# A second, turned copy of the prompt in place of TensorE transposes, in a one-core RG-LRU and HGRN2 layer

## What is computed

```
hn = rmsnorm(x, pre_w) * (1 + scale) + shift       # over D = 1024
xa, ga, q, fr, iv, gb = split(hn @ w_in)           # 6 x 512 columns
ya = rglru(causal_conv(xa)) * silu(ga)             # group A
yb = rmsnorm(hgrn2(q, log f, k, v=iv)) * silu(gb)  # group B, 4 heads of 128
x  = x + gate * rmsnorm(concat(ya, yb) @ w_out, post_w)
```

## Time and profile before

| what | us |
|---|---|
| median of 3 timed runs (lowest to highest) | 954.21 (952.94 to 954.56) |
| profiled execution | 949.82 |
| span of the profiled execution | 948.0 |
| TensorE (PE) busy | 883.1 (93% of the span) |
| VectorE (DVE) busy | 681.3 (72%) |
| ScalarE (ACT) busy | 510.7 (54%) |
| GpSimd (POOL) busy | 259.5 (27%) |

### The profile page before, as it was taken

How to read it: one execution, slowest core, us unless ns; L and a number is a source line. 1 busy time by engine, 2 the same in 40 slices (tenths; PEclk the granted TensorE clock), 3 DMA queues, 4 the chain that set the end, 5 groups by cost and what they waited for, 6 DMA issues and landing times.

```text
span 948.0 us, 20981 instructions
## 1 busy us (share of the span) xinstructions
PE 883.1 (93%) x8178; PEld 650.4 (69%) x8235; DVE 681.3 (72%) x1791; ACT 510.7 (54%) x1057; POOL 259.5 (27%) x348
## 2 busy tenths in 40 slices
PE   5889948899999999999999999999999999999884
PEld 5648847468675877579666877588757966697742
DVE  3586795768677776867686877778686768587766
ACT  2665468434763367536753377436852575436531
POOL 6031345602242222313140224212241214032400
PEclk9999987999999999999999999999999999999997
DMA  9965111100110010100110011001010101010234
GB/s 364 386 255 209 46 45 45 67 2 24 46 68 1 24 46 24 45 4 21 45 68 1 24 46 67 2 23 46 20 49 1 47 1 53 2 46 1 73 107 139
DMA packets 21821, 61.19 MB, mean 65 GB/s; under 512 B 2844, under 2 KB 11888, under 8 KB 18140
## 3 DMA queue, kind: packets, MB, share of 16 engines
q1 hardware_dynamic: 21724, 59.86, 17.0%
HBM read 48.90 MB, written 10.95 MB: 63 GB/s over the span
## 4 chain that ended last, share of the span: by engine, by line
PE 53%; DVE 20%; ACT 14%; issue 8%; DMA 2%; POOL 2%; SPq 0%; DVEq 0%; ACTq 0%; POOLq 0%
PE ring L429 43%; DVE xc L1347 5%; DMA work<-in_ada_w_dram 2%; DVE qlo L1250 2%; DVE kk L1268 2%; ACT hnh L1000 2%; ACT okv L997 2%; DVE qq L1266 1%; PE okv L518 1%; ACT L972 1%; ACT aux L997 1%; ACT wih L1024 1%; PE okv L520 1%; PE okv L519 1%; DVE xc L1345 1%
## 5 line engine op out<-in xcount | busy, mean ns | idle before, releaser
L429 PE MATMUL ring<-hnh,wih 128*128 128x256 bf16 (+1 forms) x1152 | 288.9, 262 | 2.4 <-DVE hnl L1389 2.2
L429 PE MATMUL ring<-hnl,wih 128*128 128x256 f16 (+1 forms) x1152 | 288.8, 262 | 0.0
L429 PE MATMUL ring<-hnh,wil 128*128 128x256 bf16 (+1 forms) x1152 | 288.8, 262 | 0.0
L429 PE MATMUL ring<-woh,work 128*128 128x512 f16 x512 | 162.4, 379 | 1.3
L1772 POOL TENSOR_TENSOR klo<-kk,khi 128x256 bf16<-128x256 f32 x96 | 75.3, 784 | 227.6 <-ACT khi L912 227.2
L429 PEld LDWEIGHTS ring<-hnh,wih 128*128 128x128 f16 x1152 | 109.8, 98 | 15.4 <-DVE hnl L1389 2.8
L429 PEld LDWEIGHTS ring<-hnl,wih 128*128 128x128 f16 x1152 | 109.8, 98 | 11.9
L429 PEld LDWEIGHTS ring<-hnh,wil 128*128 128x128 bf16 x1152 | 109.8, 98 | 11.5
L1250 DVE TENSOR_TENSOR qlo<-qq,qhi 128x256 f16<-128x256 f32 x112 | 66.5, 593 | 67.1 <-ACT qhi L916 57.7
L912 ACT ACTIVATE khi<-kk 128x256 f16<-128x256 f32 x96 | 40.4, 421 | 115.3 <-DVE kk L1268 90.6
L429 PE MATMUL ring<-wih,hnh 128*128 128x512 f16 x256 | 97.1, 379 | 2.4 <-ACT kk L895 1.3
(11 more groups left out here) (356 smaller groups left out, 1905.2 us busy)
## 6 DMA issues: line engine op xcount, KB each, us to landing
xin<-in_x_prompt_dram SPq DMA_DIRECT2D x16, 512.0 KB, 3.6
work<-in_x_prompt_dram SPq DMA_DIRECT2D x16, 512.0 KB, 4.2
out_dram<-work SPq DMA_DIRECT2D x16, 512.0 KB, 2.6
work<-in_ada_w_dram SPq DMA_DIRECT2D x4, 1024.0 KB, 7.5
woh<-in_ada_w_dram SPq DMA_DIRECT2D x4, 1024.0 KB, 12.2
wol<-in_w_in_dram SPq DMA_DIRECT2D x4, 1024.0 KB, 13.5
work<-in_w_in_dram SPq DMA_DIRECT2D x4, 1024.0 KB, 10.1
woh<-in_w_in_dram SPq DMA_DIRECT2D x4, 1024.0 KB, 9.6
```

The lines of the kernel that those rows point to most:

```text
L429: last = mm(out, a(k), b(k), start=start and k == ks[0] and j == 0, stop=stop and k == ks[-1] and j == 2)
```

## The change

- The host puts a second layout of the prompt in memory, `x_turned`: for each body 128 partitions (columns of a block of D) by 8 x 256 tokens. From body 1 on, SyncE loads it into `xin` by one DMA of 1 MB (`load_turned`), and TensorE transposes no rows. Body 0 works as before.
- The rows are still needed for the sums of squares. They come in four parts of 128x512 through a small buffer `xs` of two parts (`load_part`); for body 1 the second tile lands in `gp`, which is free until the gate's rows are written there.
- The factors lie one to a token. `spread` makes two matmuls with a stationary operand that repeats a column of factors 128 times, and ident as the moving one: each partition of `aux[1]` then holds all 256 factors.
- `x_norm` multiplies `xin`, 128x2048, by these in one VectorE instruction, in front of `forget(n, 1)`, behind `x_out(n-1, 0)`. `x_scale` falls away but for body 0.
- The eight instructions with scale and shift now work in place in SBUF (`modulated`), and stand in pairs among the levels of the second half. `hn_out` keeps the four copies and its place, and waits for the last projection of the body.
- `x_stats` and `squares_x` of body 0 move to the place that they have in the other bodies.
- TensorE's waits on `hn_lo` in front of `turn_k`, `gates` and `unit` are replaced by waits on the gates' signals; `residual` is cut in `residual_in` and `residual_out`, with the loads of parts between them.

```diff
+        xt = xin[:, :, :].rearrange("p t d -> p (t d)").rearrange("p (k s) -> p k s", k=KT)
+        xs = sb("xs", [P, 2, 512])
...
+            def load_turned(m):
+                sp.wait_ge(*((tr_ps, 4) if m == 1 else (hn_lo.sem, hn_lo.at(m - 1, 4))))
+                sp.dma_start(xin[:, :, :].rearrange("p t d -> p (t d)"), x_turned[m]).then_inc(xtl, 16)
+
+            def load_part(m, i):
+                t, c = divmod(i, 2)
+                if m > 1:
+                    sp.wait_ge(xsq.sem, xsq.at(m, i - 1) if t else xsq.at(m - 1, 4))
+                sp.dma_start(xs[:, c, :], xp_rows[m * NT + t][:, 512 * c:512 * c + 512]).then_inc(xld[c].sem, 16)
...
+            for n in range(1, BODIES - 1):
+                residual_in(n - 1, 0)
+                load_part(n + 1, 2)
+                load_part(n + 1, 3)
+                residual_out(n - 1, 0)
+                residual_in(n - 1, 1)
+                if n + 2 < BODIES:
+                    load_part(n + 2, 0)
+                    load_part(n + 2, 1)
+                    load_turned(n + 2)
+                residual_out(n - 1, 1)
...
+            def spread(m):
+                pe.wait_ge(newt_x.sem, newt_x.at(m + 1, 0))
+                pe.wait_ge(ytl.sem, ytl.at(m - 2, 4))
+                for t in range(NT):
+                    last = mm(aux[1][:, T + P * t:T + P * t + P], xrs[:, 0, t:t + 1].to_broadcast([P, P]), ident[:, :],
+                              start=True, stop=True)
+                last.then_inc(tr_ps, 1)
...
                 unit(n, 0, 1)
+                if not last_body:
+                    spread(n + 1)
...
                 level(n, 1, 6)
-                pe.wait_ge(r_sig.sem, r_sig.at(n, 2))
-                if not last_body:
-                    turn_x(n + 1, 0)
-                    pe.wait_ge(i_sig.sem, i_sig.at(n, 2))
-                    turn_x(n + 1, 1)
-                    pe.wait_ge(yb_ok.sem, yb_ok.at(n, 4))
-                    pe.wait_ge(s_upd.sem, s_upd.at(n, 4))
-                    turn_x(n + 1, 2)
-                    turn_x(n + 1, 3)
...
-                if not last_body:
-                    pe.wait_ge(hn_lo.sem, hn_lo.at(n + 1, 4))
                 unit(n, 1, 0)
...
+            def modulated(m, j):
+                dst = xt[:, 2 * j:2 * j + 2, :] if m else x_banks[j][:, :].rearrange("p (k t) -> p k t", k=2)
+                act.wait_ge(*((xn_ok, NT + m) if m else (tr_ps, j + 1)))
...
                 q_out(n, 1)
                 weights("wi", 10)
+                following(0)
                 heads(n, 1, 1)
+                following(1)
                 heads(n, 1, 2)
                 xa_out(n, 0)
+                following(2)
                 weights("wi", 11)
                 heads(n, 1, 3)
                 ga_out(n, 0)
+                following(3)
                 heads(n, 1, 4)
...
+            def x_norm(m):
+                dve.wait_ge(tr_ps, 4 + m)
+                dve.wait_ge(xtl, 16 * m)
+                V.tensor_tensor(xt, xt, aux[1][:, T:2 * T].unsqueeze(1).to_broadcast([P, KT, T]), ALU.mult).then_inc(xn_ok, 1)
...
                 if not first:
                     x_out(n - 1, 0)
+                if not last_body:
+                    x_norm(n + 1)
                 forget(n, 1)
...
-                if first:
-                    x_stats(n + 1)
-                    x_scale(n + 1, 0, 1)
```

More of the change, by code:

```diff
@@ L344, in _ @@
                 if (kind, c) == ("ada", 8):
-                    for t in range(NT):
-                        load_x(1, t)
+                    load_turned(1)
+                    load_part(1, 0)
+                    load_part(1, 1)
+                    sp.wait_ge(pre_ps, 1)
+                    sp.dma_start(gp[:, :], xp_rows[NT + 1]).then_inc(c_ld, 16)
                 if before[kind, c]:
@@ L368, in _ @@
             sp.wait_ge(wo_lo, NWO)
[L369 to L379, removed]
+            load_turned(2)
+            load_part(2, 0)
+            load_part(2, 1)
+            for n in range(1, BODIES - 1):
[9 more added lines that the diff above has]
+                residual_out(n - 1, 1)
+            sp.wait_ge(hn_lo.sem, hn_lo.at(BODIES - 1, 4))
             sp.dma_start(xin[0:TD, 0, :], x_sample.rearrange("b l d -> (b l) d")).then_inc(d_ld, 16)
@@ L383, in _ @@
             for t in range(NT):
-                residual(BODIES - 2, t)
+                residual_in(BODIES - 2, t)
+                residual_out(BODIES - 2, t)
             sp.wait_ge(dv("proj_ps"), 1)
@@ L468, in turn_x @@
                                                    xin[:, t, P * k:P * k + P], ident[:, :])
-                last.then_inc(tr_ps.sem, 1)
+                last.then_inc(tr_ps, 1)
             def turn_y(n, j):
@@ L1030, in weights, with following @@
                             head(kind, c)
+                def following(j):
+                    if not last_body:
+                        modulated(n + 1, j)
                 weights("wi", 3)
@@ L1048, in body @@
                     heads(n, 0, 3 + t)
-                    if not (first or last_body):
+                    if not last_body:
                         squares_x(n + 1, t)
@@ L1055, in body @@
                     squares_d()
-                elif not first:
+                else:
                     squares_x(n + 1, 2, 3)
@@ L1136, in _ @@
             act.wait_ge(mod_ok, 1)
+            modulated(0, 0)
             hn_out(0, 0)
+            modulated(0, 1)
             hn_out(0, 1)
@@ L1140, in _ @@
             act.wait_ge(mod_ok, 2)
+            modulated(0, 2)
             hn_out(0, 2)
+            modulated(0, 3)
             hn_out(0, 3)
@@ L1554, in _ @@
             x_stats(0)
-            x_scale(0, 0, 1)
+            x_scale()
             dve.wait_ge(mod_ps, 3)
```

74 lines of the change are left out of this document (44 added, 30 removed).

## The result

| | before | after |
|---|---|---|
| median of the timed runs, us | 954.23 (952.94 to 954.56) | 942.05 (940.88 to 942.89) |
| profiled execution / its span, us | 949.82 / 948.0 | 940.88 / 939.2 |
| TensorE, VectorE, ScalarE busy, us | 883.1, 681.3, 510.7 | 872.4, 677.3, 511.4 |

The kernel after takes 0.9882 of the time before, 95% interval 0.9863 to 0.9902: faster by 12.2 us, where 2.9 us were forecast.

The account below looks back on a forecast made before the run. It took the VectorE-ScalarE chain from level 2 through the tail, not TensorE, to bind. Bodies 1 to 6: 6 x (0.82 - 1.24) = -2.5 us, body 0 -0.4, together -2.9; with 4.39 us offset, 951.3 us, range 945.6 to 957.3.

Parts of the forecast that it names:

- the pairs lie under ScalarE's waits: Four pairs of `modulated` among the second half's levels, about 1.0 us each, costed at nothing because ScalarE waits there.
- the cover in front of level 2: Level 2's operand waited 0.84 us for TensorE, `forget` 0.21 us for q; this much VectorE delay was to stay hidden.
- so only 0.4 us are gained: VectorE ahead of `forget`: without `x_scale` (1.41 us) the units' norm still waits for ScalarE's last sum, so gains only 0.4 us.
- the term x: How much later the silu comes in a body, through `x_norm` ahead of `forget`: 0.82 us, from 0.22 to 1.7.
- the tail, 1.24 us: Body's gain before x: `unit` 1.04 us earlier behind the silu, plus 0.2 us of waiting for the last gate gone.
- body 0, "-0.4 us": Body 0's change with its sums moved into the first half: -0.4 us, between -2.5 and +1.3.
- three pairs less on ScalarE ahead of `k_out`: In body 0, three scale-and-shift pairs leaving ScalarE: 3 us against 1.3 us late, giving back 1.7 us.
- the 1.3 us: Body 0's delay remaining at level 7: second half 2.3 us late, less 1.0 us of ScalarE's idle time.
- the offset of 4.39 us: Median of the runs shown, 954.21 us, above the profiled execution, 949.82; added to the forecast 946.9 to give 951.3 us.
- TensorE as the bound: Rival: TensorE bounds the kernel after all, so seven bodies give 15 us together, 939.4 us; chance 0.05.
- `x_norm` costs more than the tail gives: Rival: `x_norm` ahead of the levels makes x over 1.24 us, 957 to 958.3 us at x = 1.7; chance 0.15.
- The half rate in each body's gap: Rival: TensorE's idle gap before the silu brings back 1.2 GHz, up to 1008 us; chance 0.03.

Follow-up runs that it names:

- idle transposes: Sixteen transposes of ident that nothing reads, put back on TensorE behind level 6 of bodies 0 to 6 of the kernel after; 943.64 us, ratio to before 0.9886.

## Why the prediction fell short

**What held.** That the transposes stand off the chain (0.48 of 1.78 us show), that TensorE would wait for the silu on `ring[1]` (1.12 us), that `hnl` no longer holds the `unit`, that `x_norm` takes 2.3 us, that the pairs lie under ScalarE's waits, and that the cover in front of level 2 is 0.84 + 0.21 us (1.19 measured). The clock stayed at 1.00, 2.4 GHz, through the new gap in the body shown.

**First step that failed: "so only 0.4 us are gained", the term x.** It put `forget` 1.87 us later and left x = 0.82 beyond the cover. The 0.4 us were the start of the norm alone. Without `x_scale` most of the norm also got out of the way of `bounds`, and norm and `x_out` took 7.85 us in place of 9.22, 1.37 us less (9.17 again with `x_norm` ahead of them); so `forget` came only 0.4 us later in the body, and VectorE's part of x was nothing. The earlier trace rows did not show the slow steps, and the prediction did not ask which of VectorE's steps stood beside GpSimd. What was left of x is `spread`: priced at 0.22 us from the transposes' 1.78 / 16, it cost 0.45 us, as its two matmuls stand as four of 0.11 us in the trace (L485 x4). x was 0.41 us, not 0.82: 6 x 0.41 = 2.5 us.

**Second: the tail, 1.24 us, measured 1.73.** The mechanism was right; the size was short by 0.17 us up to the `unit` and by 0.32 us behind it. The first is the price of `gates`: the sum took the 1.89 us that they last in the trace, but the next matmul starts 1.73 us behind their start (455.51 to 457.24), and that distance is what they cost. The second is two waits of TensorE's weight loads that the sum left out and that went as well: at the first pair of the `unit` (0.33 us to the next start in place of 0.22) and at the next turn of y, for VectorE's `gbs` (0.32 in place of 0.11).

**Third: body 0, "-0.4 us", measured -3.7.** The silu ended 0.88 us late (141.61 against 140.73), near the forecast 1.3; but behind it "three pairs less on ScalarE ahead of `k_out`", priced at 3 us, gave 4.6: from the silu's end to the first mark 19.50 us before and 14.92 after. The sum also took the 1.3 us off twice: 3 - 1.3 = 1.7 is net already, so by its own terms body 0 was -1.7. One of the prediction's own signs of being wrong, body 0 moving by more than 2.5 us, came true. TensorE's timeline before and after:

```profile
144.73 2.04 PE L538 MATMUL aux<-xc,wg 128*128 128x256 f32 x4 [0.59 <-DVE hnl L1389]
147.61 2.07 PE L538 MATMUL aux<-xc,wg 128*128 128x256 f32 x4 [0.84 <-ACT ktr L926]
149.85 0.80 PE L518 MATMUL okv<-vv,am 128*128 128x128 f32 x2 [0.17 <-DVE hnl L1389]
```

```profile
144.38 2.80 PE L569 MATMUL aux<-xc,wg 128*128 128x256 f32 x8
147.02 0.38 PE L547 MATMUL okv<-vv,am 128*128 128x128 f32 x2
```

Before, the two parts of the gates and the `unit` each wait; after, they run without a stop. The granted clock of these stretches, before and then after:

```profile
133.00:152.50 19.50, 10.78 (x44) 8.14 (x44) 11.32 (x20) 14.13 (x24) 7.59 (x8) 0.50 0.16 54
```

```profile
133.00:146.00 13.00, 5.16 (x28) 4.74 (x29) 11.22 (x21) 6.90 (x10) 4.85 (x5) 0.50 0.21 81
146.00:156.50 10.50, 9.34 (x77) 8.15 (x76) 5.16 (x22) 10.36 (x22) 6.58 (x7) 0.99 0.28 102
```

In half-microsecond windows the clock stays at 0.50, 1.2 GHz, until 153.0 before and until 146.0 after, and is at 1.00 from 153.5 and 146.5 on. The Trainium skill (TensorE: Matmul & The Clock Gate, What's actually happening) has it that idleness brings the half rate and activity ends it; the rows agree here, and the prediction used the rule for the wrong place, the short gap in each body, and not for body 0, whose clock it had already read as 0.50. That the pairs' leaving causes this is shown from two sides: with the pairs back in the tail the stretch takes 19.4 us (142.74 to 162.16), and with the sums moved alone 19.2 (141.75 to 160.92). In all six profiles with the pairs among the levels and the silu behind the root it takes 14.9 us, and in the second profile of before 21.5. Of the 4.6 us, 1.2 lie ahead of the gates, 2.5 in them and 1.4 in the `unit` behind them, which pays 0.43 us for a pair of matmuls at the lower clock and 0.22 at the higher; 0.6 are given back later. Up to the second part of the gates it is the wait for ScalarE's `ktr` that sets the time, and not the clock: in the second profile of before the first part took 1.10 us in place of 2.04, and the second part still started 6.88 us behind the silu's end, as in the first. How the rest parts between waits and clock is not settled.

**Fourth: the offset of 4.39 us.** I carried it from the profiled execution of before to the forecast. The second profile of before shows part of where it comes from, body 0, whose end moved by 3.5 us between two executions; against that profile body 0 would have gained 7.2 us and not 3.7. After, the profiled execution lies 1.2 us under the median. So the timed gain (12.2 us) exceeds that of the profiled executions (8.9). Against it, the profiled tail of after was long: in 8.5 us of it (886.5 to 895.0) the clock was 0.80 (1.00 in the same stretch of before), which is 8.5 x 0.2 = 1.7 us by estimate, and the last store took 3.6 us to land in place of 2.6. The stretch behind the last mark takes 164.0 to 166.8 us in the nine other profiles of kernels with the change, and 164.0 to 165.8 in the four without it: it varies with the execution, and no run shows that the change has a part in it.

**The rivals.** TensorE as the bound would have given 939.4 us, near the measured time, and is wrong all the same: the idle transposes show 0.48 us of 1.78. That `x_norm` costs more than the tail gives falls with x. The half rate in each body's gap did not come; its price was not added up right either (six bodies of 10.7 us less 2.9 are +61 us and not +57, and a tenth of that would end near 957 us and not over 960).

**The sum by its own terms.** Forecast 6 x -0.42 - 0.4 = -2.9 us; measured up to the last mark 6 x -1.31 - 3.7 = -11.5 us, close to the timed 12.2; in part that closeness is luck, as it hangs on which execution of before was profiled. Of the 8.6 us that are missing, x has 2.5, the tail 2.9 and body 0 3.3.

## What to carry to other kernels

When work leaves an engine, ask not only when its own chain ends but what its neighbour's small steps were slowed by: here five of seven small steps no longer stood beside GpSimd, which the forecast had left out. What an instruction costs is not its length but its length less the wait that follows it: sixteen transposes of 1.78 us cost 0.48 us in front of a wait of 1.30 us and 1.78 us without it, and one line, the silu ahead of the root, was worth as much per body (1.30 us) as the whole change. Before a layout is rebuilt to relieve an engine, look for the one wait that it stands in front of.

## What was unexpected of the hardware

Steps of 0.16 us on one column took up to 1.10 us beside GpSimd, while a product of 128x2048 with its factors in PSUM kept its 2.28 us; with the factors in SBUF it took 2.48 us, and GpSimd's instruction beside it 3.19 us in place of 1.16. And TensorE's half rate was no matter of the start alone: in the middle of body 0 the granted clock was 0.50 from 133.0 to 153.0 before, where the gates waited twice, and from 133.0 to 146.0 after, where they did not; in the second profile of the same kernel before it came in two stretches, until 145.5 and from 149.0 to 159.0. What decides how long it lasts is not shown.
